# A two-block transformer kernel: the last expert's gate inside its lows, columns between sums back, and the queries of the second block finished last

## The reference, cut to what matters

```python
def first_block(...):            # its end
    h = h + g2[:, None, :] * hier_moe(u2, ...)      # experts: silu(a) * b * gate, then w2
    return rmsnorm(h, norm_final_g)

def second_block(x, p, norm_gain, w_in, ...):
    xn = rmsnorm_2(h, norm_gain[i]).astype(dt)
    proj = xn @ w_in[i]
    aq, ak, av, ag, bq, bf, bi, bg, gate_a, gate_b = jnp.split(proj, split_pts, axis=-1)
    ya = moba_attention(qa, ka, va, rel_bias)        # 8 heads, softmax over 256 keys
    ya = (ya * jax.nn.silu(ag)).astype(dt) @ w_up_a[i]
    log_f = jax.nn.log_sigmoid(fpre) + ...           # fpre is bf, the forget gates
    kb = (1.0 - lb) * jax.nn.sigmoid(-fpre)
    qb = jax.nn.silu(bq)                             # the queries
    yb = hgrn2_chunkwise(qb, kb, vb, log_f)          # vb is bi
    yb = (rmsnorm_2(yb, ...) * jax.nn.silu(bg)).astype(dt) @ w_up_b[i]
    merged = sigmoid(gate_a) * ya + sigmoid(gate_b) * yb
    h = h + merged @ w_out[i]
    h = h + (p[i] @ w_ple[i]) * sigmoid(h @ w_ple_gate[i])
```

## Time and profile before

| | us |
|---|---|
| median of 3 runs | 735.8 (735.67 to 735.87) |
| the profiled execution, its own time | 736.06 |
| its span | 734.3 |
| PE busy | 711.9 (97%) |
| DVE busy | 515.1 (70%) |
| ACT busy | 380.3 (52%) |

### The profile page before, as it was taken

One profiled execution on the slowest core, in us unless ns is written; L12 is line 12 of the kernel. 1 busy time (PEld: TensorE's weight loads), 2 busy tenths in 40 slices (PEclk: granted clock), 3 DMA queues, 4 the chain that ended last, 5 costly groups with the idle time before them and its releaser, 6 DMA issues.

```text
span 734.3 us, 9981 instructions
## 1 busy us (share of the span) xinstructions
PE 711.9 (97%) x3798; PEld 575.7 (78%) x3798; DVE 515.1 (70%) x761; ACT 380.3 (52%) x549; POOL 40.5 (6%) x52
## 2 busy tenths in 40 slices
PE   4999999999999999999999999989999999999997
PEld 2887666768888877888878777769888887888886
DVE  1456897546677774875668988987998665656854
ACT  3334435554536344564357877748534547644442
POOL 0002110010020000000000000011003400000000
PEclk9999999999999999999999999999999999999999
DMA  9999688588346931756679999945544574545541
GB/s 283 348 282 384 241 304 299 198 318 312 116 144 211 359 118 57 233 187 187 197 241 334 367 357 362 375 167 155 150 130 136 164 219 141 172 135 186 169 140 58
DMA packets 104893, 164.06 MB, mean 223 GB/s; under 512 B 10896, under 2 KB 53613, under 8 KB 104718
## 3 DMA queue, kind: packets, MB, share of 16 engines
q1 hardware_dynamic: 102942, 155.54, 63.9%
q0 software_dynamic: 1904, 7.90, 3.2%
HBM read 162.33 MB, written 1.08 MB: 223 GB/s over the span
## 4 chain that ended last, share of the span: by engine, by line
PE 82%; DVE 9%; ACT 3%; DMA 3%; issue 1%; SPq 0%; POOL 0%; ACTq 0%; DVEq 0%; POOLq 0%
PE p L559 23%; PE p L561 22%; PE p L560 22%; DVE s_rawr L1844 3%; PE p L628 2%; PE p L617 2%; PE p L1234 2%; DMA s_raw<-in_w_gate_dram 2%; PE p L698 1%; PE p L674 1%; DMA s_GS<-in_w_ada_dram 1%; PE p L1063 1%; ACT s_hi L1395 1%; ACT s_L L1445 1%; PE p L686 1%
## 5 line engine op out<-in xcount | busy, mean ns | idle before, releaser
L1844 DVE TENSOR_TENSOR s_rawr<-s_raw,s_hi 128x1024 fp32r<-128x1024 f32 x240 | 287.0, 1224 | 47.6 <-ACT s_hi L1395 46.9
L1395 ACT ACTIVATE s_hi<-s_raw 128x1024 fp32r<-128x1024 f32 x240 | 245.5, 1055 | 115.5 <-PE p L561 47.7
L559 PE MATMUL p<-s_hi,s_Ah 128*128 128x512 f32 (+1 forms) x464 | 187.3, 404 | 1.1 <-DVE s_rawr L1844 0.7
L561 PE MATMUL p<-s_hi,s_Al 128*128 128x512 f32 (+1 forms) x464 | 179.7, 387 | 0.0
L560 PE MATMUL p<-s_rawr,s_Ah 128*128 128x512 f32 (+1 forms) x464 | 179.4, 387 | 0.0
L559 PEld LDWEIGHTS p<-s_hi,s_Ah 128*128 128x128 f32 x464 | 87.2, 188 | 28.8 <-issue 8.8
L561 PEld LDWEIGHTS p<-s_hi,s_Al 128*128 128x128 f32 x464 | 87.1, 188 | 18.5
L560 PEld LDWEIGHTS p<-s_rawr,s_Ah 128*128 128x128 f32 x464 | 87.4, 188 | 15.9 <-issue 0.5
L559 PE MATMUL p<-s_hi,s_Bh 128*128 128x512 f32 x192 | 76.3, 397 | 0.5 <-DVE s_BI L2411 0.3
L561 PE MATMUL p<-s_hi,s_Bl 128*128 128x512 f32 x192 | 75.0, 391 | 0.0
L560 PE MATMUL p<-s_rawr,s_Bh 128*128 128x512 f32 x192 | 74.8, 390 | 0.0
(11 more groups left out here) (377 smaller groups left out, 850.1 us busy)
## 6 DMA issues: line engine op xcount, KB each, us to landing
s_raw<-in_w_in_dram SPq DMA_DIRECT2D x80, 512.0 KB, 4.7
s_raw<-in_w_exp_gate_dram SPq DMA_DIRECT2D x64, 256.0 KB, 4.1
s_raw<-in_w_exp_up_dram SPq DMA_DIRECT2D x64, 256.0 KB, 5.0
s_raw<-in_w_exp_down_dram SPq DMA_DIRECT2D x32, 512.0 KB, 5.7
s_GS<-in_w_ada_dram SPq DMA_DIRECT2D x12, 1024.0 KB, 7.4
s_raw<-in_w_gate_dram SPq DMA_DIRECT2D x16, 512.0 KB, 9.5
s_GS<-in_w_ada_dram SPq DMA_DIRECT2D x8, 512.0 KB, 9.2
s_raw<-in_w_ret_out_dram SPq DMA_DIRECT2D x8, 512.0 KB, 3.6
```

What stands on the lines that cost most here:

```text
L559: pe.matmul(o, xh, wh, start=start, stop=False)
L561: return pe.matmul(o, xl, wh, start=False, stop=stop)
L1395: act.activation(T.hi[:, i % NHL, :], T.raw[:, i % NRAW, :], ACT.Copy).then_inc(*S.hi(i))
L1844: dve.tensor_tensor(T.lo[:, i % NRAW, :], T.raw[:, i % NRAW, :], T.hi[:, i % NHL, :].bitcast(F32), ALU.subtract).then_inc(*S.lo_dve(i))
```

## The change

In the order of the program:

- Experts' end: of the four highs and lows ahead of expert 15's `silu` and `hidden`, two (`dn15`) move behind them, on ACT and on DVE.
- Joint: `u3_cols(0)` moves ahead of `rows_back(2, 1)`, and `u3_cols(4)` and `u3_cols(6)` both move behind the third turned piece. DVE's `gated(0, tt)` moves ahead of the second pair of columns.
- Pieces: bq0, bq1, bf0, bf1, bf2, bf3, bq2, bq3, where it was bq0 to bq3, then bf0 to bf3. The PSUM banks of all later chunks swap pairs.
- ACT and DVE take the forget gates first and the queries last. ACT does Silu of the queries behind two highs that follow the sigmoids. DVE's first `queries(1)` also waits for that Silu now, as `level(0)` on PE does.
- `av`'s last piece stands between the transposes of the attention's queries and those of its keys.
- ACT: two highs ahead of the first Exp, two behind it, then `prob`, then `silu_normed("ag")`, which stood ahead of `prob`.

The diff, cut to what is named above:

```diff
@@ -88,7 +88,8 @@
             some(f"up{e}", range(4))
         if e:
             some(f"dn{e - 1}", range(2))
-    for name in SECOND:
+    some("bq", (0, 1)), some("bf", range(4)), some("bq", (2, 3))
+    for name in SECOND[2:]:
         some(name, range(4))
     for n in range(2):
         some(f"ub{n}", range(2)), some(f"ua{n}", range(2))
@@ -105,7 +106,8 @@
 CHUNKS = ["dq", "rq", "rk", "rv0", "rv1", "rg0", "rg1", "ga0", "ga1", "gb0", "gb1", "do0", "do1", "ro0", "ro1", "wo0", "wo1"]
 PAIR = {name: (i + 1) % 2 for i, name in enumerate(CHUNKS)}
-PAIR.update({name: i % 2 for i, name in enumerate(SECOND + ["ub0", "ua0", "ub1", "ua1", "wu0", "wu1", "pg0", "pg1"])})
+PAIR["bq"], PAIR["bf"] = 0, 1
+PAIR.update({name: (i + 1) % 2 for i, name in enumerate(SECOND[2:] + ["ub0", "ua0", "ub1", "ua1", "wu0", "wu1", "pg0", "pg1"])})
 LEVEL_AFTER = [0, 1, 3, 4, 6, 7, 9, 10, 11]
@@ -1172,6 +1174,11 @@
             q.wait_ge(*S.dve_rows.at("lo", 0, 1))
         down(n, 0, (0, 1), (f"dn{n}", 0, 1))
         down(n, 1, (0, 1), (f"dn{n}", 1, 1))
+
+    def u3_cols(k0):
+        q.wait_ge(*S.dve_moe.at("x3", min(k0 // 2, 2), 1))
+        turn(lambda tt, k: T.X3[:, tt, 128 * k:128 * k + 128], ("u3", k0), S.dve_cols.at("u3", k0))
+
     hidden_cols(15)
     q.wait_ge(*S.dve_rows.at("lo", 1, 1))
     rows_back(0, 0), rows_back(1, 0)
@@ -1180,28 +1187,24 @@
         down(15, 0, (c,), None)
         down(15, 1, (c,), ("dn15", c, 1))
     rows_back(2, 0)
-    rows_back(0, 1), rows_back(1, 1), rows_back(2, 1)
+    rows_back(0, 1), rows_back(1, 1)
+    t_free[0] = t_free[1] = S.dve_moe.at("lo", 15)
+    u3_cols(0)
+    rows_back(2, 1)
+    u3_cols(2)
     m_free[0] = m_free[1] = S.dve_moe.at("gy", 1, 1)
     z_free[0] = z_free[1] = [S.dve_rows.at("lo", 2, 1)]
     z_free[2] = z_free[3] = [S.dve_moe.at("gy", 0, 1)]
-    t_free[0] = t_free[1] = S.dve_moe.at("lo", 15)
-
-
-    def u3_cols(k0):
-        q.wait_ge(*S.dve_moe.at("x3", min(k0 // 2, 2), 1))
-        turn(lambda tt, k: T.X3[:, tt, 128 * k:128 * k + 128], ("u3", k0), S.dve_cols.at("u3", k0))
+
     def u3(h):
         return "u3", 2 * h
-    u3_cols(0), u3_cols(2)
-    uses("bq", 0, 1, A, u3, turned=True)
-    u3_cols(4)
-    uses("bq", 1, 2, A, u3, turned=True)
-    u3_cols(6)
-    uses("bq", 2, 4, A, u3, turned=True)
-    chunk_freed("bq", S.dve_hgrn.at("bq", 0), S.dve_hgrn.at("bq", 1))
-    uses("bf", 0, 2, A, u3, turned=True)
+    uses("bq", 0, 2, A, u3, turned=True)
+    uses("bf", 0, 1, A, u3, turned=True)
+    u3_cols(4), u3_cols(6)
+    uses("bf", 1, 4, A, u3, turned=True)
+    chunk_freed("bf", S.dve_hgrn.at("bf", 0), S.dve_hgrn.at("bf", 1))
     b = turn_bank("norm")
     q.wait_ge(*S.pool_moe.at("r2"))
@@ -1209,14 +1212,14 @@
         r = pe.transpose(PT[b][:, 128 * tt:128 * tt + 128], T.r2[:, tt:tt + 1].broadcast_to([128, 128]), ident)
     r.then_inc(*S.turned("norm", 0))
     t_free[b] = S.dve_moe.at("norm row")
-    uses("bf", 2, 4, A, u3, turned=True)
-    chunk_freed("bf", S.dve_hgrn.at("bf", 0), S.dve_hgrn.at("bf", 1))
+    uses("bq", 2, 4, A, u3, turned=True)
+    chunk_freed("bq", S.dve_hgrn.at("bq", 0), S.dve_hgrn.at("bq", 1))
     def level(lv):
         qa, ka = (T.T1, T.T2) if lv == 0 else (T.qks[1][0], T.T2) if lv == 1 else T.qks[lv % 2]
         nq = 128 if lv == 0 else 64
         if lv == 0:
-            q.wait_ge(*S.act_hgrn.at("bf", 1))
+            q.wait_ge(*S.act_hgrn.at("bq", 1))
         else:
             q.wait_ge(*S.dve_hgrn.at("q", lv))
         if lv > 1:
@@ -1263,13 +1266,13 @@
     uses("bg", 2, 4, A, u3)
     chunk_freed("bg", S.act_moba.at("bg", 0), S.act_moba.at("bg", 1))
     hgrn_out(1)
-    uses("av", 0, 2, A, u3)
-    uses("av", 2, 3, A, u3)
+    uses("av", 0, 3, A, u3)
     for name, z in (("aq", T.ZC[0]), ("ak", T.ZC[1])):
         q.wait_ge(*S.dve_moba.at("norm", name, 1))
         for k0 in (0, 2):
             turn(lambda tt, k: z[:, tt, 128 * k:128 * k + 128], (name, k0), S.dve_moba.at(name, k0))
-    uses("av", 3, 4, A, u3)
+        if name == "aq":
+            uses("av", 3, 4, A, u3)
     chunk_freed("av", S.act_copy.at("av"), S.dve_copy.at("av"))
     def moba_logits(tt, g):
@@ -1366,8 +1369,8 @@
     h_cols(6)
     uses("pg0", 2, 4, B, hT)
     for tt in range(2):
-        bank = PZ[2 + tt]
-        for w in z_free[2 + tt]:
+        bank = PZ[2 * PAIR["pg1"] + tt]
+        for w in z_free[2 * PAIR["pg1"] + tt]:
             q.wait_ge(*w)
         for h in range(4):
             wh, wl = wview(AT["pg1", h], 2)
@@ -1703,10 +1706,11 @@
         hid_high(n)
         if n == 1:
             third_high()
-        his_to(AT[f"up{n + 2}", 2] if n < 14 else AT["dn15", 1] + 1)
+        his_to(AT[f"up{n + 2}", 2] if n < 14 else AT["dn15", 0])
     silu(15)
+    his_to(AT["dn15", 1] + 1)
     hid_high(15)
-    his_to(AT["bq", 2])
+    his_to(AT["bf", 0])
     rows_out(2, 0), rows_out(2, 1)
@@ -1715,10 +1719,8 @@
         squares(S.act_moe, ("sq " + key,), src, junk, c, n, tt)
     cols_scaled("u3", 0, T.Ah, T.g_in2), cols_scaled("u3", 2, T.Ah, T.g_in2)
-    his(1)
-    cols_scaled("u3", 4, T.Ah, T.g_in2)
-    his(1)
-    cols_scaled("u3", 6, T.Ah, T.g_in2)
+    his_to(AT["bf", 2])
+    cols_scaled("u3", 4, T.Ah, T.g_in2), cols_scaled("u3", 6, T.Ah, T.g_in2)
     his(1)
     for n in range(2):
         for tt in range(2):
@@ -1762,11 +1764,11 @@
         q.wait_ge(*S.act_moe.at("sq x", 1, tt))
         act.activation(T.X[:, tt, :], T.X3[:, tt, :], ACT.Copy, scale=T.r1[:, tt:tt + 1]).then_inc(*S.act_moe("xf", tt))
     his(1)
-    heads("bq", "bq", T.T1, T.T1, ACT.Silu, 1.0)
-    his(2)
     heads("f", "bf", T.T2, T.fA, ACT.Sigmoid, 1.0)
     q.wait_ge(*S.act_hgrn.at("f", 1))
     heads("bf", "bf", T.T2, T.T2, ACT.Sigmoid, -1.0)
+    his(2)
+    heads("bq", "bq", T.T1, T.T1, ACT.Silu, 1.0)
     his_to(AT["ak", 0])
     copy_normed("bi", T.BV[:, 0, :], banks("bi")[0])
     his_to(AT["bg", 0])
@@ -1786,12 +1788,12 @@
     copy_normed("av", T.AV[:, 0, :], banks("av")[0])
     his_to(AT["sa0", 2])
     cols_scaled("yb", 0, T.Bh, T.g_hg, 4), cols_scaled("yb", 2, T.Bh, T.g_hg, 4)
+    his_to(AT["sa1", 0])
     exps(S.act_moba, S.dve_moba, 0)
-    his(1)
+    his_to(AT["sa1", 2])
+    prob(S.act_moba, S.pe_moba, "moba", 0, 1)
     silu_normed("ag", lambda tt: T.RGS[:, 1, 512 * tt:512 * tt + 512])
-    his(2)
-    prob(S.act_moba, S.pe_moba, "moba", 0, 1)
-    his(2)
+    his_to(AT["sa1", 3])
     gate_second("sa0")
     his(2)
     exps(S.act_moba, S.dve_moba, 1)
@@ -2447,7 +2449,7 @@
         hid_low(n)
         if n == 1:
             third_low()
-        lows_to(AT[f"up{n + 2}", 2] if n < 14 else AT["dn15", 1] + 1)
+        lows_to(AT[f"up{n + 2}", 2] if n < 14 else AT["dn15", 0])
         if n == 2:
             q.wait_ge(*S.final_gain_in.at(0))
             q.wait_ge(*S.dve_ada.at(11))
@@ -2459,8 +2461,9 @@
             q.wait_ge(*S.masks_in.at(0))
             dve.tensor_copy(T.masks[:, :, :], T.G1[:, :].rearrange("p (l t) -> p l t", l=8)).then_inc(*S.dve_moe("masks"))
     hidden(15)
+    lows_to(AT["dn15", 1] + 1)
     hid_low(15)
-    lows_to(AT["bq", 2])
+    lows_to(AT["bf", 0])
     rows_out(2, 0), rows_out(2, 1)
@@ -2492,18 +2495,18 @@
     for j in range(2):
         rows_in(j, 0), rows_in(j, 1)
-    gated(1, 0)
     cols_scaled("u3", 0, T.Ah, T.Al, T.g_in2)
-    residual(1, 0)
+    gated(0, 0), gated(0, 1)
+    cols_scaled("u3", 2, T.Ah, T.Al, T.g_in2)
+    gated(1, 0), residual(1, 0)
+    lows_to(AT["bf", 1])
     gated(1, 1), residual(1, 1)
-    cols_scaled("u3", 2, T.Ah, T.Al, T.g_in2)
-    lows_to(AT["bq", 3])
+    lows_to(AT["bf", 2])
     cols_scaled("u3", 4, T.Ah, T.Al, T.g_in2)
-    lows_to(AT["bf", 0])
     cols_scaled("u3", 6, T.Ah, T.Al, T.g_in2)
-    gated(0, 0), gated(0, 1)
+    lows_to(AT["bf", 3])
     residual(0, 0), residual(0, 1)
-    lows_to(AT["bf", 2])
+    lows_to(AT["bq", 2])
     v = st[:, 488:496].rearrange("p (s n t) -> p s n t", s=2, n=2)
     q.wait_ge(*S.act_moe.at("sq x", 1, 1))
     dve.tensor_tensor(st[:, 496:500].rearrange("p (s t) -> p s t", s=2), v[:, :, 0, :], v[:, :, 1, :], ALU.add).then_inc(*S.dve_moe("sum"))
@@ -2512,7 +2515,7 @@
     q.wait_ge(*S.dve_moe.at("norm1"))
     dve.scalar_tensor_tensor(out=st[:, 504:506], in0=st[:, 498:500], scalar=1.0 / 1024.0, in1=st[:, 502:504],
                              op0=ALU.mult, op1=ALU.add).then_inc(*S.dve_moe("norm2"))
-    lows_to(AT["bf", 3])
+    lows_to(AT["bq", 3])
     def normed(name, dst):
@@ -2528,9 +2531,10 @@
     q.wait_ge(*S.turned.at("norm", 0))
     dve.tensor_copy(T.r2row, T.PT[T.turn_bank["norm",]][:, 0:256]).then_inc(*S.dve_moe("norm row"))
     q.wait_ge(*S.dve_moe.at("norm row"))
+    normed("bf", T.T2)
+    lows_to(AT["bi", 1])
     normed("bq", T.T1)
     lows_to(AT["bi", 2])
-    normed("bf", T.T2)
     def blocks(a, B, half):
         return a.rearrange("p h (n a b) -> p (h n) a b", a=2, b=B)[:, :, half, :]
@@ -2542,6 +2546,8 @@
         q.wait_ge(*S.act_hgrn.at("f", 1))
         if lv > 1:
```

(2 more changed lines are left out.)

## The result

| | before | after |
|---|---|---|
| median of 10 runs each, us | 735.73 (735.40 to 736.76) | 738.03 (737.51 to 739.66) |
| profiled execution, own time | 736.06 | 738.34 |
| its span | 734.3 | 736.7 |
| its mean granted clock | 1.000 | 0.995 |

The ratio is 1.0031 (95% interval 1.0022 to 1.0040): the changed kernel is 2.3 us slower. The forecast was 736.0, in a range from 734.0 to 737.8, so it was wrong: the measured median lies 0.2 us above that range.

What follows compares the result with a forecast made beforehand. PE was taken as the bound, busy 711.9 of 734.3 us. The terms +2.0 - 0.8 - 1.0 gave +0.2 us on the profiled 736.06, 736.26, so a median of 736.0, range 734.0 to 737.8.

Steps and rivals of the forecast that it cites:

- Expert 15: At expert 15's transposes: with two lows ahead of `hidden`, PE waits for nothing, 0.9 us gained.
- Columns between the sums back: In the joint: the first turned piece starts about 5.6 us behind `rows_back(2, 0)`, a lead of 1.6 us.
- Third piece ahead, and where the lead goes: Joint and gates: lead grows to 2.5 us, then PE's waits of 0.7, 0.45 and 0.3 cut it to about 1.1.
- The queries last: ACT's chain before `level(0)`: an added table load makes it start 2.0 us later, PE idle about 3.2 us.
- the sign: What would show the forecast right: a wait of PE of about 3 us at L1236 for ACT's L1737.
- The later gains don't come: Rival at the attention: waits at the second logits and L698 stay, both gains gone, median 737.8; chance 0.12.
- DVE's lag: In the levels: `queries(1)` starts 3.2 us later, DVE 0.8 us further behind PE, taken in by its idle time.
- `av` and `prob`: At the attention: `av`'s piece between the transposes gains 0.8 us; `prob` ahead of Silu gains 1.0 us at L698.
- The drain of the table load: At ACT's added table switch: the skill's drain of about 1380 ns was left out; with it the sum would be +1.6.

Runs made afterwards that it cites:

- e6: Kernel before with only expert 15's new order of highs and lows on ACT and DVE: 735.10 us against 736.48, ratio 0.9984.
- e1: Changed kernel plus 26 identity transposes on PE ahead of the wait at `level(0)`: 736.12 us against 736.78 for the kernel before, ratio 0.9991.
- e4: Kernel before with only ACT's new gate order, queries' Silu last, DVE following, pieces in old order: 741.73 us, ratio 1.0078.
- e5: Kernel before with expert 15's new order, `av`'s last piece between the transposes, and `prob` ahead of `ag`'s Silu: 733.07 us against 736.48, ratio 0.9958.
- e3: Changed kernel with Sigmoid in place of Silu for the queries, so without the added table load: 734.57 us against 736.78 for the kernel before, ratio 0.9978.

## Why the prediction was wrong

- **Expert 15: right.** No wait at L1108; 0.9 us in the trace and -1.2 us (-1.8 to -0.5) timed in e6.
- **Columns between the sums back: right.** The first piece starts at 487.39, 5.55 us behind `rows_back(2, 0)` at 481.84, as worked out. Its lead on the kernel before is 1.72 behind H (predicted 1.6).
- **Third piece ahead, and where the lead goes: right.** PE waits 0.57 and 0.24 for the lows, where three waits of 0.7, 0.45 and 0.3 were worked out; from start to start of the matmuls the two cost 1.3 us against 1.45. PE ends the first piece of `bi` near H+45.3 (predicted 516.7, H+45.14).
- **The queries last: the mechanism and the size of the wait were right, its price was not.** L1765 is 0.61 us later behind H (0.7 predicted), the chain from ACT's first high to the end of the Silu takes 519.31 - 498.18 = 21.13 us (21.02), the added load is 1.28, PE's wait is 3.21 (3.2; the sign named L1236, the row is L1237's) and `level(0)` starts 2.01 later (2.0).
- **The failed step is the one that follows: "`level(0)` starts at 520.0, 2.0 us later than before, with PE idle for about 3.2 us in front of it. So everything gained up to here is given back and 2.0 us more."** That priced a wait of PE at its idle time. Behind this wait the granted clock was 0.50 for some 6 us in the profiled execution, and PE needed 2.93 us more for the same instructions. No term and no rival held this; the rows had a clock of 1.00 throughout, in a kernel in which PE is never idle for over 1.2 us in this stretch, so they could say nothing of what a longer wait brings. e1 takes just this away and gets 0.9991; e4 has it without the rest of the change.
- **A rival's number came close by luck.** "The later gains don't come" had a median of 737.8, near the measured 738.03. But both gains came (0.96 and 1.06 in the trace, e5 in time), and what stands in their place is the clock.
- **DVE's lag: right.** `queries(1)` starts at H+48.52 (519.41), 3.27 us later (3.2), and from 529 to 560 PE is busy throughout.
- **`av` and `prob`: right.** 0.96 and 1.06 won, for 0.8 and 1.0 (eight transposes take 0.79 from start to start, not 0.85); e5 confirms all three of the gains in time.
- **The drain of the table load: rightly left out.** The second load takes 1.28 us, starts 0.02 behind the end of the high (514.86 + 1.99 = 516.85), and the Silu starts 1.29 behind it. The rule of the Trainium skill ("ScalarE: Activation LUTs", section "What ACT_TABLE_LOAD costs") of a drain of some 1380 ns besides is not in this trace, and e3, without the load, wins 1.42 us at `level(0)`, so the drain has no room there either.

The sum, put right: +2.01 + 2.93 - 0.96 - 1.06 + 0.13 = +3.05 us in the profiled execution. The medians differ by 2.3. The executions differ in how long the low clock lasts: the changed kernel's mean clock is 0.997 or 0.998 in its six runs up to 738.1 and 0.995 in the four above. With only the two levels, a mean of 0.998 over 736 us is about 3 us at the lower one, and 0.995 about 7 (an estimate; the figures have three digits). So 2.93 us is the price in the profiled execution, one of the four at 0.995, and in the other six it was by this estimate about half of that. With that price the sum is about +1.6 us in them, at the lower end of what was timed (1.6 to 2.9). What decides its length in a run stays open.

## What to carry to other kernels

A wait on a busy TensorE can cost twice: its idle time, and a lower clock behind it. Where a change makes one that is longer than any in the old trace, price both, and ask what fills it. Before an engine's chain is made longer, look for its idle time just ahead of the chain's start: here ScalarE stood for 6.93 us there, and filling it, with the Silu moved ahead of one high, turned +2.3 us into -4.4.
